# Two mixer layers at the end of an eight-part network kernel: transposes two slots later, stick heads one per slot, a gate product as a step of its own, operand tiles through two banks

## The reference

```
for layer in range(2):                       # stages 4 and 5
    h = rmsnorm(x, norm_g[layer])
    parts = split(h @ w_in[layer], 8)        # 8 parts of 256 columns
    if layer == 0:  ...dilated mixture and block attention, gated by silu...
    else:
        qc, kc, vc, gc, qd, kd, vd, gd = parts
        oc = diff_attention(rope(qc), rope(kc), vc)   # per head: p0 - lambda * p1, then @ v, rmsnorm
        od = stick_breaking(qd, kd, vd)               # per head: z, log(1 - sigmoid(z)), suffix sums, exp, @ v
        y = concat([oc * silu(gc), od * silu(gd)])
    x = x + y @ w_out[layer]
return rmsnorm(x, final_norm_g)
```

## Time and profile before

| | us |
|---|---|
| median of 3 runs (2849.96 to 2853.24) | 2851.08 |
| the profiled execution, its own time | 2848.9 |
| its span, from the first instruction to the last | 2847.0 |
| PE busy | 2796.8 |
| DVE busy | 1585.5 |
| ACT busy | 1357.5 |
| POOL busy | 223.2 |

### The profile page before, as it was taken

How to read it: one execution, slowest core, us unless ns; L and a number is a source line. 1 busy time by engine, 2 the same in 40 slices (tenths; PEclk the granted TensorE clock), 3 DMA queues, 4 the chain that set the end, 5 groups by cost and what they waited for, 6 DMA issues and landing times.

```text
span 2847.0 us, 32926 instructions
## 1 busy us (share of the span) xinstructions
PE 2796.8 (98%) x13534; PEld 2323.8 (82%) x13534; DVE 1585.5 (56%) x1870; ACT 1357.5 (48%) x1975; POOL 223.2 (8%) x197
## 2 busy tenths in 40 slices
PE   9999999999999999999999999999999999999998
PEld 7788888778888888888888888888888888887777
DVE  6665776756455454444644556654544544466656
ACT  6554355545444444333634544644444443355565
POOL 0112324400000000000010001000000000000002
PEclk9999999999999999999999999999999999999999
DMA  7755544565666666555655443566666665564533
GB/s 222 136 130 130 101 111 104 127 207 180 191 189 192 185 188 191 190 192 189 217 170 156 126 123 128 187 192 192 190 189 185 190 192 191 190 206 162 167 116 132
DMA packets 213350, 480.83 MB, mean 169 GB/s; under 512 B 15312, under 2 KB 16336, under 8 KB 212560
## 3 DMA queue, kind: packets, MB, share of 16 engines
q1 hardware_dynamic: 210848, 467.57, 56.7%
q0 software_dynamic: 2352, 11.17, 1.1%
HBM read 476.58 MB, written 2.10 MB: 168 GB/s over the span
## 4 chain that ended last, share of the span: by engine, by line
PE 87%; DVE 5%; ACT 4%; issue 2%; DMA 1%; POOL 1%; ACTq 0%; POOLq 0%; SPq 0%; DVEq 0%
PE PS L1053 18%; PE PS L1055 18%; PE PS L1054 18%; PE PS L1102 7%; PE PS L1101 7%; PE PS L1100 7%; DVE WL L2029 2%; ACT WH L1568 1%; DVE WORK L2162 1%; PE PS L1214 1%; PE PS L1431 1%; PE PS L1128 1%; PE PS L1311 1%; PE PS L1227 1%; PE PS L1226 1%
## 5 line engine op out<-in xcount | busy, mean ns | idle before, releaser
L2029 DVE TENSOR_TENSOR WL<-RAW,WH 128x1024 fp32r<-128x1024 f32 x827 | 1034.5, 1253 | 989.9 <-ACT WH L1568 988.7
L1568 ACT ACTIVATE WH<-RAW 128x1024 fp32r<-128x1024 f32 x831 | 875.9, 1055 | 832.5 <-PE PS L1055 514.6
L1053 PE MATMUL PS<-WH,UTH 128*128 128x512 f32 x2396 | 958.8, 400 | 9.0 <-DVE WL L2029 8.9
L1055 PE MATMUL PS<-WH,UTL 128*128 128x512 f32 x2396 | 937.7, 391 | 0.0
L1054 PE MATMUL PS<-WL,UTH 128*128 128x512 f32 x2396 | 936.7, 391 | 0.0
L1053 PEld LDWEIGHTS PS<-WH,UTH 128*128 128x128 f32 x2396 | 451.9, 189 | 104.6 <-DVE WL L2029 11.9
L1055 PEld LDWEIGHTS PS<-WH,UTL 128*128 128x128 f32 x2396 | 451.4, 188 | 97.7
L1054 PEld LDWEIGHTS PS<-WL,UTH 128*128 128x128 f32 x2396 | 452.5, 189 | 87.5
L1102 PE MATMUL PS<-WH,HTL 128*128 128x512 f32 x656 | 259.3, 395 | 0.0
L1101 PE MATMUL PS<-WL,HTH 128*128 128x512 f32 x656 | 258.8, 394 | 0.0
L1100 PE MATMUL PS<-WH,HTH 128*128 128x512 f32 x656 | 255.4, 389 | 0.0
(11 more groups left out here) (406 smaller groups left out, 2541.1 us busy)
## 6 DMA issues: line engine op xcount, KB each, us to landing
RAW<-in_ffn_w_gu SPq DMA_DIRECT2D x352, 512.0 KB, 4.2
RAW<-in_ffn_w_down SPq DMA_DIRECT2D x176, 512.0 KB, 4.5
RAW<-in_ab_w_in SPq DMA_DIRECT2D x128, 512.0 KB, 4.7
RAW<-in_nsa_w_in SPq DMA_DIRECT2D x80, 512.0 KB, 3.7
RAW<-in_w_in SPq DMA_DIRECT2D x64, 512.0 KB, 3.9
RAW<-in_ab_w_out SPq DMA_DIRECT2D x32, 512.0 KB, 4.3
RAW<-in_nsa_w_out SPq DMA_DIRECT2D x32, 512.0 KB, 3.9
RAW<-in_w_out SPq DMA_DIRECT2D x16, 512.0 KB, 4.6
```

Source lines behind the costliest of these rows:

```text
L1053: e.matmul(o, lh, wh[:, j], start=k + j == 0, stop=False)
L1055: x = e.matmul(o, ll, wh[:, j], start=False, stop=k + j == NKT - 1)
L1568: e.activation(wh, raw, ACTF.Copy).then_inc(*a_hi.inc(s))
L2029: e.tensor_tensor(wl, raw, wh.bitcast(F32), ALU.subtract).then_inc(*v_lo.inc(s))
```

## The change

In stage 5 the transposes `df_t` stand two slots behind `df_a` instead of one. The scores of the stick heads, `st_z`, are put one head per slot, and `st_l`, `st_m`, `st_a` and `st_w` follow later, in pairs. The three last products of `y2d` on DVE become a step `y2g` one slot later, and `ot(5,0)` waits for that one. In stages 4 and 5 `ot` puts its two k tiles into two banks, with a copy and a subtraction of 256 columns for each, and the output matmul of tile k waits for its own half. By the generators, the new list is:

```diff
@@ def diff(h, i):
         put("df_a", h, i)
-        yield
+        yield from pause(2)
         put("df_t", h, i)
@@ def close_diff():
         put("y2d")
         yield
+        put("y2g")
+        yield
@@ def stick(h):
-        yield from pause(1 + h // 2)
+        yield from pause(1 + h)
         put("st_z", h)
-        yield from pause(2 - h // 2)
+        yield from pause(4 - h + h // 2)
         put("st_l", h)
         yield
         put("st_m", h)
-        yield from pause(2 + h // 2)
+        yield from pause(2)
         put("st_a", h)
@@ mixer(5, ...)
-          operand(5, 0, ("y2d",), behind=4), operand(5, 2, *[("st_o", h) for h in range(4)]))
+          operand(5, 0, ("y2g",), behind=4), operand(5, 2, *[("st_o", h) for h in range(4)]))
@@ tensor: row
-                    on.wait_ge(*v_ut.of("ot", st, k - k % 2))
+                    on.wait_ge(*v_ut.of("ot", st, k if st > 2 else k - k % 2))
@@ tensor: ot
                 for j in range(2):
+                    if st > 2:
+                        b = b if j == 0 else take("ot", st, k + 1)
                     for t in range(2):
-                        x = e.transpose(b[:, 256 * j + 128 * t:256 * j + 128 * t + 128], operand_of(st, k + j, t), ident)
-                x.then_inc(*p_ut.inc("ot", st, k))
+                        c = 128 * t if st > 2 else 256 * j + 128 * t
+                        x = e.transpose(b[:, c:c + 128], operand_of(st, k + j, t), ident)
+                    if j or st > 2:
+                        x.then_inc(*p_ut.inc("ot", st, k + j if st > 2 else k))
@@ scalar: ot
+                if st > 2:
+                    for kk in (k, k + 1):
+                        on.wait_ge(*p_ut.of("ot", st, kk))
+                        e.activation(UTH[:, kk], banks.ap("ot", st, kk)[:, 0:256], ACTF.Copy).then_inc(*a_ut.inc("ot", st, kk))
+                    return
@@ vector: ot
+                if st > 2:
+                    for kk in (k, k + 1):
+                        on.wait_ge(*a_ut.of("ot", st, kk))
+                        e.tensor_tensor(UTL[:, kk], banks.ap("ot", st, kk)[:, 0:256], UTH[:, kk].bitcast(F32),
+                                        ALU.subtract).then_inc(*banks.empty(v_ut, "ot", st, kk))
+                    return
@@ vector: y2d
                 rstd(ss, ss, 64, 1.0 - LAMBDA, "y2d")
+
+            @step
+            def y2g():
+                y = Y2[:, :, 0:256]
+                ss = ST2[:, 64:72]
                 on.wait_ge(*g_rs.of("r", "y2d"))
```

More of the change, by code:

```diff
@@ L937, in build @@
         row_slots = {st: [a[4] for a in ORDER if a[0] == "row" and a[1] == st] for st in KTILES}
-        last_ot = {a[1]: a[2] for a in ORDER if a[0] == "ot"}
+        last_ot = {a[1]: a[2] + (a[1] > 2) for a in ORDER if a[0] == "ot"}
         col_end = {(a[1], a[2]): a[4] for a in ORDER if a[0] in ("col", "nar")}
@@ L2503, in y2d @@
             def y2d():
-                y = Y2[:, :, 0:256]
                 ss = ST2[:, 64:72]
```

## The result

| | before | changed | ratio, 95% interval |
|---|---|---|---|
| median of 11 runs each | 2851.55 us (2849.64 to 2853.94) | 2845.17 us (2841.35 to 2848.55) | 0.9977, 0.9967 to 0.9986 |
| the profiled execution, span | 2847.0 us | 2839.7 us | |

The medians are 6.4 us apart, 0.22%; the forecast was 6.7 us and 2844.4 us. A second set of the changed kernel gave 0.9983 (0.9974 to 0.9992), 2844.55 against 2850.53 us. So the time is less, and whether by more or less than 0.2% these sets don't decide. The two profiled spans differ by 7.3 us, and not all of that is the change: the two executions were already 1.7 us apart in stage 4, ahead of PE's wait for UTL there. Up to slot 852 the granted clock was at 0.50 for 17.1 us in the execution before and for 10.2 us in the changed one.

The account below looks back on a forecast made before the run. PE, busy 98% of the span, was taken as the bound, so only its own work or waits count. Gains of 9.2 us less costs of 2.5 net 6.7 us, forecast 2844.4 us, range 2841.5 to 2848.5.

Parts of the forecast that it names:

- Slot 865: Stage 5, stick heads one per slot: slot 865 can start 3.0 us earlier, 1.3 of its 3.22 us wait staying.
- The clock: At slot 865 the granted clock stays at full speed after a 1.3 us wait: 2.4 us gained.
- the argument from the 1.41: Matmuls kept normal pace after both ot waits of 1.41 us, so a 1.3 us wait should keep the clock.
- The transposes: Stage 5, df_t two slots behind: no longer meets a running df_a, 1.0 us gained at head 3.
- Fewer switches: df_o and st_a share a line, saving two changes of PE and a small mask wait: 0.5 us gained.
- The banks: PE waits for PSUM banks: 0.6 us for df_s(2) in line 860, 0.65 for st_a(0) in line 868.
- y2g: DVE step split off: 0.9 us gained at slot 872 with the switch, 0.6 lost at slot 873.
- The upper bound of 2.7: Largest cost allowed for late y2g before slot 873, against 0.6 expected; as a rival, chance 0.12.
- The table load: One more ACT table load before the last gate2 makes PE wait in slot 876: 1.25 us lost.
- The rival by the Trainium skill: Each table switch also carries a 1.4 us drain, slot 876 waiting for it too: 2845.8 us, chance 0.02.
- Operand tiles: Stages 4 and 5, ot in two banks: each wait for UTL 0.7 us shorter, 1.4 us gained.
- Two of the signs that the prediction named: Slot 865 waits about 1.3 us with the clock at 1.00; slot 873 waits at most 0.6 us.

Follow-up runs that it names:

- e2: Changed kernel with the stick heads put where they were before; stretch from slot 852 to the last matmul 117.67 us, against 116.13 in the changed kernel.
- e7: Changed kernel with the stick heads two by two, in lines 861 and 863; stretch from slot 852 115.86 us, against 116.13.
- e4: Changed kernel with y2g directly behind y2d, without the yield between them; stretch from slot 852 119.26 us, against 116.13.
- e3: Changed kernel with the transposes df_t one slot behind again; stretch from slot 852 117.55 us, against 116.13.
- e6: As e5, with gate2(5,1) also moved behind the last exp of the stick heads, to line 870; stretch from slot 852 112.84 us.
- e5: Changed kernel with y2g two lines later, in line 872; stretch from slot 852 114.66 us, against 116.13.
- e1: Changed kernel with the order of before, leaving only the operand tiles in two banks; stretch from slot 852 120.15 us, against 120.80 before.
- e9: Changed kernel itself, run again on one chip; median 2844.55 us over 11 runs, ratio 0.9983 against the kernel before, stretch 116.17 us.

## Why the prediction was right, and where its terms were off

The direction, the time and most of the mechanism held. By its steps:

*Slot 865.* That ACT and DVE take turns, and that the stick heads between the exps and WH were what delayed it, is shown by e2. The weights came as early as forecast: counted from the start of slot 852, which is 2.7 us earlier in the changed execution, WL of 865 was to be ready at 2763.7 and was at 2763.44. What failed is the other half: PE was to come at 2765.1 less the shift of 2.7, that is 2762.4, and wait 1.3; it came at 2764.35 and waited 0. The step had counted the stick heads as the same work for PE wherever they stand. One head alone costs 0.93 us of PE (slot 861 takes 3.79 where a slot after side work takes 2.86), while before two heads and three transposes together cost 1.27 (slot 861: 4.13), because the scores of two neighbouring heads run at the same time. One head per slot gives that up twice: e7 restores it, and PE's own time falls by 1.5. A bank wait of 0.3 us in line 860 comes on top. So the wait that was to remain was there as PE's own time instead, and a larger one: 2.4 us gained, not 3.0.

*The clock.* It stayed at 1.00 through slot 865; the 2.4 us were gained in full. In e2 and e4 it fell at waits of 3.20 and 2.83 us and cost 1.6 and 1.45 us. In stage 5 it fell at no wait of 1.41 us or less in any of the twelve profiles, so the argument from the 1.41 held here; the last section has a place where a shorter wait was enough.

*The transposes.* 1.0 us forecast, 1.4 measured in e3, 0.9 of it at the transposes of head 3. Both parts of the order are needed.

*Fewer switches.* The 0.5 us was not tried by itself. The part from slot 865 to 872, in which it stands, gained 4.4 us with 4.15 forecast.

*The banks.* In line 860 slot and side work take 5.88 us, 5.34 before, with `df_t(0)` of 0.25 now in it: 0.3 us of waiting, 0.6 forecast. In line 868 0.65 was forecast and e6 shows 0.44.

*y2g.* The wait of 0.83 at slot 872 went, and the one that comes instead was named: WL of 873 behind products held up by the power and the masks. It is mis-sized, 1.20 and with the switch 1.4 instead of 0.6, not because of the power, which took 2.70 where the step had 1.64 and 1.2 more, but because the products behind it took 1.28 and 0.83, 2.1 us in all, where the step had 1.75. WL of 873 behind them took 1.48 instead of 1.2, with POOL's last mask running until 2793.65, and the power began 24.1 us after the start of slot 865 where the step had 23.8. The upper bound of 2.7 held. e4 shows that without the split it would have been far worse, and e5 that two lines later it is free. The rule of the Trainium skill (SBUF — State Buffer, 🔬 SBUF: two separate sides), that a DVE operation with two SBUF inputs and a GpSimd operation that reads SBUF exclude each other and the later one waits for the whole instruction of the other, agrees with the 2.70 of the power: 1.64 and most of the 1.23 of a WL.

*The table load.* 1.25 forecast, 1.42 in e6. The rival by the Trainium skill (ScalarE: Activation LUTs, What ACT_TABLE_LOAD costs), a switch of about 2.66 us, did not come: gate2 starts 1.30 after its table load starts, and PE waits 1.36. The measurement decides against the drain as an addition here.

*Operand tiles.* 0.7 twice forecast, 0.65 and 0.7 measured (e1).

Together the change is worth 5.4 us by its stretch, 6.7 forecast; the medians say 6.4 and 6.0. So the net sum was 1.3 us too large: 0.6 for PE's own time before slot 865, 0.8 around slot 873 and 0.2 at the table load, less 0.3 in between. That the median came within 0.8 us of 2844.4 us is in part luck, since one set's difference between medians (6.4 us) is larger than what the stretch accounts for (5.4 us). Two of the signs that the prediction named did not come: slot 865 did not wait 1.3 us, and slot 873 waited more than 0.6.

## What to carry to other kernels

Here ACT and DVE took turns, and a side task queued on either of them ahead of its part of the next weights delayed all the weights that followed. Spread such tasks over the slots, but look first at what they share on TensorE: two heads whose 64-row scores stand directly behind each other ran at the same time, and putting them apart cost PE 1.5 us (e7). Look at what an order does to the sequence of activation functions. Before, a table load at 2777.67 was followed by 2.96 us of idle ACT and cost nothing; where a PSUM bank waited behind it, as in slot 876, it cost PE 1.42 us (e6). And a step that waits for POOL cost nothing once it stood two lines later, out of the way of the next weights (e5: 1.5 us).

## What the runs showed that I had not expected

The two programs are the same ahead of stage 4, and yet they run differently there. In stage 2, PE waits 1.08 us, up to 1623.17 and 1622.20, in both executions (L1427 before, L1433 changed, the same instruction), and in one of them the clock falls behind it. The waiting matmul and the stretches behind it, before and changed (columns as in the earlier trace rows):

```profile
1623.17 1.15 PE L1427 MATMUL PS<-WORK,BIG 15*128 15x128 f32 x8 [1.08 <-ACT BIG L1913]
...
1624.00:1626.00 2.00, 2.00 (x8) 1.51 (x8) 1.61 (x4) 0.57 (x2) 0.00 (x0) 0.73 0.75 242
1626.00:1628.00 2.00, 2.00 (x6) 1.60 (x5) 0.46 (x1) 1.50 (x7) 0.00 (x0) 0.50 0.00 1
```
```profile
1622.20 1.15 PE L1433 MATMUL PS<-WORK,BIG 15*128 15x128 f32 x8 [1.08 <-ACT BIG L1924]
...
1624.00:1626.00 2.00, 2.00 (x11) 1.63 (x10) 1.46 (x4) 0.47 (x2) 0.00 (x0) 1.00 0.43 165
```

The twelve matmuls of the slot behind it take 4.44 us before (1624.25 to 1628.69) and 2.87 us in the changed kernel (1623.28 to 1626.15). All twelve profiles have this wait, and the clock falls behind it in nine of them; it does not in the first profile of the changed kernel, in e3 and in e6. In e9, which is the changed kernel once more, it does. So the same wait of 1.08 us, in the same program, can be followed by 1.2 GHz or not. Its length alone does not tell: a wait of 1.74 us near 1703 goes with a fall in all twelve, one of 2.13 us near 1731 in none, and the 1.36 us in slot 876 in none of the six profiles that have it. The prediction had two waits of 1.41 us from one execution to go by, which was thin.

Such falls are a part of why the start of slot 852 lies between 2714.95 and 2719.48 in the twelve profiles, while the stretches behind it repeat within 0.05 us for equal kernels, and of the scatter of the times of one kernel, which is up to 10 us (e9: 2843.03 to 2853.24). The earliest start, in the first profile of the changed kernel, has 10.2 us at the low clock ahead of it; the others have 17.1 or 20.5. That is not all of it, since starts with 17.1 us still differ by 2.4 us. What decides for or against a fall was not tried here and stays open.
